# A decoder layer with linear attention and a 32-expert MoE: splits of weights moved into earlier phases, the bias product in one pass, row tiles turned in their own chunk

## The chip, the cores and the metric

The program runs on one core of one Trainium2 chip. The metric is the time of one execution on the device, in microseconds (us); a run's time is compared with the times of the kernel before. Engines: TensorE (matmul and transposes), VectorE (DVE), ScalarE (ACT), GpSimd (POOL), SyncE (SP, which issues transfers).

## What is computed

One layer over 2048 tokens of width 1024, all in float32. After a modulation by a condition vector there is a mixer with gated linear attention and retention heads, then a top-4-of-32 mixture of experts:

```python
h = rmsnorm(x, norm1) * (1 + sc1) + sh1
x = x + g1 * hybrid_mixer(h, ...)          # ends in  o @ w_out
h = rmsnorm(x, norm2) * (1 + sc2) + sh2
logits = hf @ w_router + b_router
top_val, top_idx = lax.top_k(logits, TOP_K)
weights = jax.nn.softmax(top_val)
gate, up = split(xs @ w_gu[e] + b_gu[e])
act = (clip(up, -7, 7) + 1) * (min(gate, 7) * sigmoid(1.702 * min(gate, 7)))
out = (act @ w_down[e] + b_down[e]) * weight      # added to the token's row
x = x + g2 * y;  return rmsnorm(x, norm_f)
```

## The kernel before

Five phases run one after the other, each a block with a program for every engine, and between two phases the semaphores are cleared behind a barrier: modulation, projection (`phase_projection`), mixer (`phase_mixer`), routing (`phase_routing`), experts (`phase_experts`), and a finish. A product of two float32 matrices is made of three matmuls over rounded parts (`split_product`, L113 to L115): hi by hi, hi by lo, lo by hi. ScalarE makes the hi part (a copy to float32r), VectorE the lo part (the value less its hi part).

**Mixer.** 16 turns of 128 tokens. SyncE loads `early` and `late` halves of the projections (L743 to L752) and stores the mixed rows (L757); a late load waits until the tile before last is gated (`out`, L965). VectorE's turn: masks, decayed q and k, `output` of the tile before (L965), state updates (L997, L1004), differences, a reduction (L1011). The output weight w_out is loaded here (L766), 4 MB, and used in the next phase.

**Routing.** First w_out is split: ScalarE four times 128x2048 (L1235), VectorE four times (L1285), with the output norm as factor. Then 16 turns, software-pipelined. TensorE's turn i: product of tile i + 1 with w_out in two halves (L113 to L115), into which are set the transposes of h2 (L1458), the router's product (L1466), the ranks (L1472, L1473) and the transpose of the routing weights W (L1476); then the transposes of tile i + 2's rows (L1436) and the bias product W x b_down (L1483), in plain float32. ScalarE splits the turned rows (L1242), then copies the turned W (L1247). VectorE: x2 from the product (L1340), lo parts (L1301), x added (L1345), yi = bias product x g2 + x2 (L1308, L1309) for the tile before, h2 (L1352, L1354), the list of places (L1314 to L1333), logits and top 4, W. Before the turns it waits for eight setup transfers:

```python
            dve.wait_ge(setup_dma, 8 * 16)
            own(nc.vector.scalar_tensor_tensor(out=A2[:], in0=A2[:], ...
```

POOL stores yi and scatters the places. After the last turn VectorE builds a table of groups (from L1384) and SyncE stores it.

**Experts.** A group is up to four tiles of 128 rows of one expert. SyncE streams its weights in 24 pieces of 512 KB (L1623) through eight buffers: six chunks (four of w_gu, two of w_down) of four pieces. ScalarE and VectorE split each piece (L1689, L1782). TensorE runs chunk by chunk, and in a chunk tile by tile, eight slices of three matmuls each. POOL gathers the rows of the next group (L1644). TensorE turns them (`rows`, L1901, eight transposes into one pair of banks), ScalarE and VectorE split them (L1694, L1788). The first row tile of the next group is turned in chunk 4, two others in the first tile of chunk 5, the fourth behind it:

```python
                                    if c == NGU + 1 and t == 0 and s in (1, 6):
                                        next_rows(s // 4 + 1)
```

At the start of the phase four pieces are split and all tiles of the first group (three here) turned one after the other before the first product.

## Time and profile before

| | |
|---|---|
| median of 3 runs | 4271.72 us (4270.05 to 4272.08) |
| the profiled execution | 4266.8 us, its span 4265.2 us |
| TensorE, VectorE, ScalarE, POOL busy | 93%, 56%, 36%, 14% of the span |
| granted TensorE clock, mean | 0.965 of full speed |
| mixer, routing, experts begin at | 749, 966, 1343 us; the finish at 4212 us |
| weight pieces split in the experts | 840, so 35 groups of 24 |
| transfers | 763 MB, 179 GB/s over the span |

A busy TensorE is not one at its peak, since the ends of matmuls are modelled. The granted clock has two levels, 1.0 (2.4 GHz) and 0.5 (1.2 GHz); a number between them is the mean over a stretch. Durations are of this one profiled execution.

### The profile page before, as it was taken

The page shows a single profiled execution, that of the slowest core. Times are in us where ns is not written, and L with a number is a line of the kernel's source. Part 1 is how long each engine was busy: PE and PEld are TensorE (multiplying, and loading weights), DVE is VectorE, ACT ScalarE, POOL GpSimd, SP SyncE. Part 2 cuts the span into 40 slices and gives each one's busy share as a digit, 9 for nine tenths or more (in the row PEclk, how much of TensorE's full clock was granted, in tenths as well). Part 3 has the DMA queues.
Part 4 walks back from the last instruction along what each step waited for, and adds up shares of the span by engine and source line. Part 5 has one row for each costly group of instructions (what it writes and reads, how often), then busy time and mean ns, then how long its engine had stood idle before and what let it go on. Part 6 is the DMA issues. An engine that isn't in the chain of part 4 may idle for free. (4 is left out here: it accounts for less than half of the span.)

```text
span 4265.2 us, 64554 instructions
## 1 busy us (share of the span) xinstructions
PE 3946.6 (93%) x18376; PEld 3224.3 (76%) x18377; DVE 2371.9 (56%) x3651; ACT 1525.0 (36%) x2203; POOL 590.1 (14%) x616
## 2 busy tenths in 40 slices
PE   6998999897994999999999999999999999999993
PEld 4887788785773877877887878877888788888773
DVE  4262342685665575464476476576556566544653
ACT  3222321562211353342245254355334434322432
POOL 1110110001222110110121011021011111110101
PEclk8999999998996999999999999999999999999997
DMA  5432441653224586464588477588567667544735
GB/s 216 166 112 95 145 146 59 236 202 131 104 94 145 151 262 221 133 213 138 150 260 266 118 261 241 178 264 283 174 192 230 188 193 235 173 128 113 248 111 182
DMA packets 340786, 763.09 MB, mean 179 GB/s; under 512 B 29274, under 2 KB 29332, under 8 KB 336068
## 3 DMA queue, kind: packets, MB, share of 16 engines
q1 hardware_dynamic: 279972, 591.52, 40.6%
q0 software_dynamic: 57680, 160.07, 14.3%
q10 hardware_dynamic: 3056, 10.53, 0.6%
q8 instruction: 41, 0.67, 0.1%
q14 instruction: 37, 0.30, 0.0%
HBM read 653.68 MB, written 108.33 MB: 179 GB/s over the span
## 5 line engine op out<-in xcount | busy, mean ns | idle before, releaser
L1689 ACT CAST exp_w_hi<-exp_w_raw 128x1024 fp32r<-128x1024 f32 x840 | 861.2, 1051 | 943.3 <-PE exp_bank_acc L115 834.7
L113 PE MATMUL exp_bank_acc<-exp_w_hi,exp_x_hi 128*128 128x512 f32 x2528 | 999.7, 395 | 14.4 <-DVE exp_w_lo L1782 12.2
L1782 DVE TENSOR_TENSOR exp_w_lo<-exp_w_raw,exp_w_hi 128x1024 fp32r<-128x1024 f32 x840 | 978.4, 1217 | 59.0 <-ACT exp_w_hi L1689 52.7
L115 PE MATMUL exp_bank_acc<-exp_w_hi,exp_x_lo 128*128 128x512 f32 x2528 | 988.2, 391 | 0.0
L114 PE MATMUL exp_bank_acc<-exp_w_lo,exp_x_hi 128*128 128x512 f32 x2528 | 987.4, 391 | 0.0
L113 PEld LDWEIGHTS exp_bank_acc<-exp_w_hi,exp_x_hi 128*128 128x128 f32 x2528 | 476.7, 189 | 115.9 <-issue 15.5
L115 PEld LDWEIGHTS exp_bank_acc<-exp_w_hi,exp_x_lo 128*128 128x128 f32 x2528 | 476.4, 188 | 101.6
L114 PEld LDWEIGHTS exp_bank_acc<-exp_w_lo,exp_x_hi 128*128 128x128 f32 x2528 | 477.3, 189 | 95.7
L113 PE MATMUL exp_bank_acc<-exp_w_hi,exp_a_hi 128*128 128x512 f32 x1264 | 506.7, 401 | 12.6 <-DVE exp_a_lo L1840 9.3
L115 PE MATMUL exp_bank_acc<-exp_w_hi,exp_a_lo 128*128 128x512 f32 x1264 | 493.6, 391 | 0.0
L114 PE MATMUL exp_bank_acc<-exp_w_lo,exp_a_hi 128*128 128x512 f32 x1264 | 493.2, 390 | 0.0
L1671 POOL DMA_INDIRECT y_rows<-exp_act_row,exp_token x123 | 196.2, 1595 | 2117.1 <-DVE exp_act_row L1852 2073.6
L113 PE MATMUL pro_bank_acc<-pro_w_hi,pro_h_hi 128*128 128x512 f32 x896 | 355.8, 397 | 0.0
L115 PE MATMUL pro_bank_acc<-pro_w_hi,pro_h_lo 128*128 128x512 f32 x896 | 350.9, 392 | 0.0
L114 PE MATMUL pro_bank_acc<-pro_w_lo,pro_h_hi 128*128 128x512 f32 x896 | 350.8, 392 | 0.0
L113 PEld LDWEIGHTS exp_bank_acc<-exp_w_hi,exp_a_hi 128*128 128x128 f32 x1264 | 237.8, 188 | 71.9 <-DVE exp_a_lo L1840 21.7
L1816 DVE SCALAR_TENSOR_TENSOR exp_gate_up<-exp_bank_acc,exp_bias 128x512 f32<-128x512 f32 x158 | 108.9, 689 | 319.2 <-PE exp_bank_acc L115 318.7
L1852 DVE SCALAR_TENSOR_TENSOR exp_act_row<-exp_bank_acc,exp_share,exp_g 128x512 f32<-128x512 f32 x123 | 92.0, 748 | 331.0 <-PE exp_bank_acc L115 322.6
L115 PEld LDWEIGHTS exp_bank_acc<-exp_w_hi,exp_a_lo 128*128 128x128 f32 x1264 | 237.5, 188 | 51.0
L114 PEld LDWEIGHTS exp_bank_acc<-exp_w_lo,exp_a_hi 128*128 128x128 f32 x1264 | 238.1, 188 | 44.9
L1805 DVE TENSOR_TENSOR exp_gate_up<-exp_bank_acc,exp_bias 128x512 f32<-128x512 f32 x158 | 108.5, 686 | 262.5 <-PE exp_bank_acc L115 116.2
L1713 ACT CAST exp_a_hi<-exp_bank_ta 128x512 fp32r<-128x512 f32 x158 | 92.5, 585 | 452.2 <-PE exp_bank_ta L1909 452.2
(299 smaller groups left out, 4286.3 us busy)
## 6 DMA issues: line engine op xcount, KB each, us to landing
exp_w_raw<-in_w_gu SPq DMA_DIRECT2D x560, 512.0 KB
exp_w_raw<-in_w_down SPq DMA_DIRECT2D x280, 512.0 KB
exp_bias<-in_b_gu SPq DMA_DIRECT2D x35, 1024.0 KB
early_w_raw<-in_w_in POOLq DMA_DIRECT2D x14, 2048.0 KB, 10.8
proj<-pro_stage SPq DMA_DIRECT2D x112, 256.0 KB
pro_w_ada<-in_w_ada POOLq DMA_DIRECT2D x64, 256.0 KB, 3.3
mix_late<-proj SPq DMA_DIRECT2D x16, 768.0 KB, 6.2
mod_w_ada<-in_w_ada SPq DMA_DIRECT2D x8, 1024.0 KB, 15.8
```

Of the source, the lines that this page charges most:

```text
L113: nc.tensor.matmul(out, act_hi, w_hi, start=first, stop=False)
L114: nc.tensor.matmul(out, act_hi, w_lo, start=False, stop=False)
L115: return nc.tensor.matmul(out, act_lo, w_hi, start=False, stop=last)
L1671: pool.indirect_dma_start(out=keep["y"][c - NGU], out_offset=bass.IndirectOffsetOnAxis(ap=token[:, t:t + 1], axis=0), in_=weighted_at(c, t ...
L1689: nc.scalar.copy(whi[:, c % 2, j * SK:(j + 1) * SK], raw[:, n % RAW]).then_inc(hi_done, 1)
L1713: nc.scalar.copy(ahi[:, t, 4 * q:4 * q + 4], ta[:]).then_inc(ahi_done, 1)
L1782: nc.vector.tensor_tensor(wlo[:, c % 2, rows], raw[:, n % RAW], whi[:, c % 2, rows], ALU.subtract).then_inc(lo_done, 1)
L1805: nc.vector.tensor_tensor(gu[:, t % 2], acc[:, bank(c, t)], bias[:, column(c):column(c) + N], ALU.add).then_inc(read_done, 1)
L1816: nc.vector.scalar_tensor_tensor(out=gu[:, u], in0=acc[:, bank(c, t)], scalar=1.0, in1=bias[:, column(c):column(c) + N], op0=ALU.add, op1= ...
L1852: nc.vector.scalar_tensor_tensor(out=weighted_at(c, t), in0=acc[:, bank(c, t)], scalar=share[:, t:t + 1], in1=g2[:, cols], op0=ALU.mult, o ...
```

## The change

1. The split of w_out moves from the head of the routing into the mixer: after each of the 16 turns ScalarE makes one hi piece of 128x512 and VectorE, at the end of its next turn, the lo piece. Raw and split weights lie in tiles that routing and experts share.
2. b_down is loaded three times, one below the other, and held as hi, lo, hi (`b_down_split`, float32r); W is held as hi, hi, lo. The bias product is two matmuls of 96 rows, in float32r. W's turned copy goes ahead of the row split on ScalarE.
3. SyncE loads the first eight weight pieces of expert 0 in the routing, behind its last loads; four are split there, around the last turn. Expert 0 always counts as one tile at least, so that group 0 is expert 0's. The eight first pieces of each next expert are then loaded at the end of a group's list.
4. yi and the places' records have two buffers; the last list of places goes ahead of the last yi.
5. In the experts only the first row tile is turned ahead; the others in the first chunk of their own group, tile t + 1 after the first slice of tile t.
6. One clearing of semaphores goes.

The core of the diff:

```diff
+def pieces_of(raw):
+    return raw[:].rearrange("p a s n -> p (a s) n").rearrange("p (r s) n -> p r s n", s=SK)
+def expert_piece(A, expert, n):
+    c, rows = n // PIECES, slice(n % PIECES * SK, (n % PIECES + 1) * SK)
+    w, col = (A["w_gu"], (c % 2) * D + (c // 2) * N) if c < 4 else (A["w_down"], (c - 4) * N)
+    return w.rearrange("o e (s p) n -> p (o e) s n", p=P)[:, bass.ds(expert, 1), rows, col:col + N]
...
+            for n in range(2):
+                for c in range(2):
+                    sp.dma_start(w_out[:, n, c * GH:(c + 1) * GH], rows_of(A["w_out"])[:, n * GH:(n + 1) * GH, c * N:(c + 1) * N]
+                                 ).then_inc(w_out_in, 16)
...
+                act.wait_ge(w_out_in, 6 * 16)
+                at = bass.ds(j, 1)
+                nc.scalar.activation(w_hi[:, u, at], w_out[:, u, at], ACT.Identity, scale=o_norm[:, u:u + 1]
+                                     ).then_inc(w_hi_done, 1)
...
+                if not is_tile(i, 0):
+                    out_weights_lo(i - 1, 1 - u, j - 1 + u)
+            def out_weights_lo(t, u, j):
+                dve.wait_ge(w_hi_done, t + 1)
+                at = bass.ds(j, 1)
+                nc.vector.scalar_tensor_tensor(out=w_lo[:, u, at], in0=w_out[:, u, at], scalar=o_norm[:, u:u + 1],
+                                               in1=w_hi[:, u, at], op0=ALU.mult, op1=ALU.subtract).then_inc(w_lo_done, 1)
...
+    bd3 = k.sb("b_down_split", [3 * E, D], F32R)
...
-            sp.dma_start(bd[:], A["b_down"].rearrange("o e d -> (o e) d")).then_inc(setup_dma, 16)
+            for part in range(3):
+                sp.dma_start(bd[part * E:(part + 1) * E, :], A["b_down"].rearrange("o e d -> (o e) d")).then_inc(setup_dma, 16)
...
+            for n in range(RAW):
+                sp.dma_start(raw[:, n], expert_piece(A, 0, n)).then_inc(first_in, 16)
...
-            for c in range(2):
-                act.wait_ge(w_in, 64)
-                for n in range(2):
-                    rows = slice(n * GH, (n + 1) * GH)
-                    ins = nc.scalar.activation(whi[:, c, rows], raw[:, c, rows], ACT.Identity, scale=keep["o_norm"][:, n:n + 1])
-                ins.then_inc(whi_done, 1)
+            def first_weights_hi(n):
+                act.wait_ge(first_in, RAW * 16)
+                nc.scalar.copy(first[:, 0, n * SK:(n + 1) * SK], raw[:, n]).then_inc(first_hi, 1)
...
+                if not is_tile(i, 0):
+                    weights_t(i - 1)
                 if not is_tile(i, NT - 1):
                     split_hi(i + 1)
-                if not is_tile(i, 0):
-                    weights_t(i - 1)
...
+                if is_tile(i, NT - 1):
+                    for n in range(2):
+                        first_weights_hi(n)
...
+            act.wait_ge(setup_dma, 10 * 16)
+            nc.scalar.copy(bd3[:], bd).then_inc(bd_hi, 1)
...
-            for c in range(2):
-                dve.wait_ge(whi_done, c + 1)
-                for n in range(2):
-                    rows = slice(n * GH, (n + 1) * GH)
-                    ins = nc.vector.scalar_tensor_tensor(out=wlo[:, c, rows], in0=raw[:, c, rows], scalar=keep["o_norm"][:, n:n + 1],
-                                                         in1=whi[:, c, rows], op0=ALU.mult, op1=ALU.subtract)
-                ins.then_inc(wlo_done, 1)
-            own(nc.vector.memset(empty[:], 0))
+            own(nc.vector.memset(empty, 0))
...
-            dve.wait_ge(setup_dma, 8 * 16)
+            dve.wait_ge(setup_dma, 10 * 16)
             own(nc.vector.scalar_tensor_tensor(out=A2[:], in0=A2[:], scalar=1.0, in1=norm2[:], op0=ALU.add, op1=ALU.mult))
             dve.wait_ge(pool_set, 1)
+            dve.wait_ge(bd_hi, 1)
+            lo = slice(E, 2 * E)
+            nc.vector.tensor_tensor(bd3[lo], bd[lo], bd3[lo], ALU.subtract).then_inc(bd_lo, 1)
...
-                nc.vector.tensor_scalar(W[:], W[:], den[:], None, ALU.mult).then_inc(ev["W"], 1)
+                own(nc.vector.tensor_scalar(W[:], W[:], den[:], None, ALU.mult))
+                own(nc.vector.tensor_copy(W3[:, 0:2], W[:].unsqueeze(1).to_broadcast([P, 2, E])))
+                nc.vector.tensor_tensor(W3[:, 2], W[:], W3[:, 0], ALU.subtract).then_inc(ev["W"], 1)
             split_lo(0)
             for_tiles(dve, step)
             own.base, own.n = SETUP + NT * PER - BEFORE, 0
+            list_places(NT - 1, 1)
             first_rows(NT - 1, 1)
-            list_places(NT - 1)
...
+            for count in (tiles, groups):
+                fin(nc.vector.tensor_scalar(count[:, 0:1], count[:, 0:1], 1.0, None, ALU.max))
...
+            for n in range(2, PIECES):
+                first_weights_lo(n)
+            dve.wait_ge(first_lo, PIECES)
...
-                nc.tensor.transpose(wt[0:E, 0:P], W[:], ident).then_inc(ev["wt"], 1)
+                nc.tensor.transpose(wt[0:3 * E, 0:P], W3[:].bitcast(F32).rearrange("p a e -> p (a e)"), ident
+                                    ).then_inc(ev["wt"], 1)
...
-                                          bd[:, c * N:(c + 1) * N], start=True, stop=True)
+                                          bd3[:, c * N:(c + 1) * N], start=True, stop=True)
...
+                    for n in range(RAW, PIECES * NCH):
+                        load(n, expert)
+                    next_expert = field(sp, g + 1, EXPERT, E - 1)
+                    with sp.If(G.nT > 0):
+                        for n in range(PIECES * NCH, PIECES * NCH + RAW):
+                            load(n, next_expert)
...
-            for n in range(PIECES):
-                weights_hi(0, n, 1)
-            T0 = tiles_in(load_word(act, 0))
-            for t in range(GT):
-                with act.If(T0 > t):
-                    rows_hi(0, t)
+            rows_hi(0, 0)
...
                     for n in range(PIECES, 2 * PIECES + PIECES // 2):
+                        if n % 2 == 0 and n // 2 - 1 < GT:
+                            own_rows_hi(n // 2 - 1)
                         weights_hi(g, n, G.chunks_before(n // PIECES - 1))
...
+                            if c == 0 and n % 2 == 0:
+                                own_rows_lo(n // 2 + 1)
                             weights_lo(g, PIECES * (c + 1) + n)
+                        if c == 0:
+                            own_rows_lo(3)
...
-                                            next_rows(0)
+                                            next_row()
                                     if c == NGU and s == KD // 2:
                                         pe.wait_ge(alo_done, G.pair_tile(1, t))
-                                    if c == NGU + 1 and t == 0 and s in (1, 6):
-                                        next_rows(s // 4 + 1)
+                                    if c == 0 and s == 1 and t + 1 < GT:
+                                        own_rows(t + 1)
...
-            kw = Kit(nc, mixing, "w_out")
-            keep["w_out"], keep["w_out_in"] = kw.sb("raw", [P, 2, KD, N]), kw.sem("in")
-            keep["o_norm"] = kw.sb("o_norm", [P, 2])
+            kw = Kit(nc, mixing, "weights")
+            keep["raw"] = kw.sb("raw", [P, 2, KD, N])
+            keep["split"] = kw.sb("split", [P, 4, KD, N], F32R)
             run(phase_mixer)
+            keep["first"] = kw.sb("first", [P, 2, KD, N], F32R)
             run(phase_routing)
-            kw.clear_sems()
-        run(phase_experts)
+            run(phase_experts)
...
```

**VectorE, end of the mixer and head of the routing.** (`weights_split` is the split w_out, `rou_A` is A2.) Before:

```order
L1011 TENSOR_REDUCE mix_var<-mix_sq 128x4
L965 SCALAR_TENSOR_TENSOR mix_o_out<-mix_oc,mix_r,mix_late 128x128 x8
L725 UNCONDITIONAL_BRANCH
L1278 UNCONDITIONAL_BRANCH
L1285 SCALAR_TENSOR_TENSOR rou_w_lo<-w_out_raw,w_out_o_norm,rou_w_hi 128x2048 x4
L1288 MEMSET rou_empty 128x1024
L1289 TENSOR_SCALAR rou_col<-keep_const 128x1
L1290 CAST rou_empty<-rou_col 128x512
L1292 SCALAR_TENSOR_TENSOR rou_A<-rou_A,rou_norm 128x1024
L1301 TENSOR_TENSOR rou_o_lo<-rou_bank_tp,rou_o_hi 128x512 x2
```

Changed:

```order
L1037 TENSOR_REDUCE mix_var<-mix_sq 128x4
L1044 SCALAR_TENSOR_TENSOR weights_split<-weights_raw,mix_o_norm,weights_split 128x512 x2
L991 SCALAR_TENSOR_TENSOR mix_o_out<-mix_oc,mix_r,mix_late 128x128 x8
L744 UNCONDITIONAL_BRANCH
L1328 UNCONDITIONAL_BRANCH
L1331 MEMSET rou_yi 128x1024
L1332 TENSOR_SCALAR rou_col<-keep_const 128x1
L1333 CAST rou_yi<-rou_col 128x512
L1335 SCALAR_TENSOR_TENSOR rou_A<-rou_A,rou_h 128x1024
L1339 TENSOR_TENSOR rou_b_down_split<-rou_yi,rou_b_down_split 32x1024
L1352 TENSOR_TENSOR rou_o_lo<-rou_bank_tp,rou_o_hi 128x512 x2
```

The two last lo pieces now stand ahead of the mixer's last output, the four large ones are gone, and the bias's low part is new between A2 and the first row split.

**ScalarE, a turn in the routing's loop.** Before:

```order
L1242 CAST rou_o_hi<-rou_bank_tp 128x512 x2
L1245 REGISTER_ALU
L1246 REGISTER_ALU
L1247 COPY rou_wT<-rou_bank_wt 32x128
L1256 ACTIVATE rou_squares,rou_ssq<-rou_x 128x1024
```

Changed:

```order
L1289 CAST rou_wT<-rou_bank_wt 96x128
L1281 REGISTER_ALU
L1282 REGISTER_ALU
L1284 CAST rou_o_hi<-rou_bank_tp 128x512 x2
L1298 ACTIVATE rou_over,rou_ssq<-rou_x 128x1024
```

The copy of the turned W, which the bias product needs, went ahead of the row split.

**TensorE, first tile of a group's last chunk (before) and of its first chunk (changed).** Before:

```order
L1927 COMPARE_AND_BRANCH
L1931 ISA
L1901 MATMUL exp_bank_tx<-keep_const,exp_rows 128x128 x8
L1927 UNCONDITIONAL_BRANCH
L113 MATMUL exp_bank_acc<-exp_w_hi,exp_a_hi 128x512
```

Changed:

```order
L116 MATMUL exp_bank_acc<-weights_first,weights_split 128x512
L117 MATMUL exp_bank_acc<-weights_first,weights_split 128x512
L118 MATMUL exp_bank_acc<-weights_first,weights_split 128x512
L1998 COMPARE_AND_BRANCH
L1968 MATMUL exp_bank_tx<-keep_const,exp_rows 128x128 x8
L1998 UNCONDITIONAL_BRANCH
L116 MATMUL exp_bank_acc<-weights_first,weights_split 128x512
```

A turn of rows that stood among the products of the activations, twice there and once behind them, now stands after the first slice of a tile's first product (the operands named `weights_split` there are the rows' parts).

## Rows read from the trace of the kernel before

**Rows 1.** Windows of TensorE: stretch, its length, busy, granted clock, DMA share, GB/s
```profile
985.00:1299.00 314.00, 289.70 (x1380) 0.94 0.26 94
...
1085.00:1105.00 20.00, 18.70 (x90) 0.91 0.30 103
```

**Rows 2.** TensorE's waits over the span: us in total, times, longest
```profile
PE exp_bank_acc L113 <- DVE exp_w_lo L1782: 14.9, 14, 1.6
...
PE mix_bank_go L1084 <- DMA mix_late<-proj: 8.6, 9, 2.3
...
PE exp_bank_tx L1901 <- DVE exp_x_lo L1788: 6.8, 6, 2.0
```

**Rows 3.** Groups by line: count, busy us, mean ns of one, idle before
```profile
L115 PE MATMUL exp_bank_acc<-exp_w_hi,exp_x_lo 128*128 128x512 f32 x2528 | 988.2, 391 | 0.0
...
L1483 PE MATMUL rou_bank_tq<-rou_b_down,rou_wT 32*128 32x512 f32 x64 | 34.6, 662 | 19.0 <-ACT rou_wT L1247 19.0
...
L1285 DVE SCALAR_TENSOR_TENSOR rou_w_lo<-w_out_raw,w_out_o_norm,rou_w_hi 128x2048 fp32r<-128x2048 f32 x4 | 9.1, 2346 | 9.2 <-ACT rou_w_hi L1235 9.2
```

**Rows 4.** Order of time in the mixer: start us, length us, what [idle before]
```profile
827.35 1.43 DVE L997 SCALAR_TENSOR_TENSOR mix_gla_state<-mix_gla_state,mix_eb,mix_bank_gs 64x128 f32<-64x128 f32 x4 [3.16 <-PE mix_bank_gs L1103]
...
835.31 2.18 DVE L965 SCALAR_TENSOR_TENSOR mix_o_out<-mix_oc,mix_r,mix_late 128x128 f32<-128x128 f32 x8
...
838.42 0.33 SPq L751 DMA_DIRECT2D mix_late<-proj  x1
...
845.08 0.70 PE L1084 MATMUL mix_bank_go<-mix_gla_state,mix_qe 128*128 128x256 f32 x2 [0.66 <-DMA mix_late<-proj]
...
850.67 1.43 DVE L997 SCALAR_TENSOR_TENSOR mix_gla_state<-mix_gla_state,mix_eb,mix_bank_gs 64x128 f32<-64x128 f32 x4 [1.88 <-PE mix_bank_gs L1103]
```

**Rows 5.** Order of time in the routing
```profile
970.66 0.71 SPq L1193 DMA_DIRECT2D rou_norm<-in_norm  x1
...
984.78 0.76 PE L113 MATMUL rou_bank_acc<-rou_w_hi,rou_o_hi 128*128 128x512 f32 x1 [12.90 <-issue]
...
1016.73 1.23 DVE L1340 TENSOR_TENSOR rou_x<-rou_bank_acc,rou_g 128x1024 f32<-128x1024 f32 x1 [3.86 <-PE rou_bank_acc L115]
...
1020.88 1.23 DVE L1308 TENSOR_TENSOR rou_yi<-rou_bank_tq,rou_g 128x1024 f32<-128x1024 f32 x1 [0.25 <-PE rou_bank_tq L1483]
...
1024.60 1.23 DVE L1354 TENSOR_TENSOR rou_h<-rou_h,rou_sh 128x1024 f32<-128x1024 f32 x1
...
1036.31 1.22 DVE L1340 TENSOR_TENSOR rou_x<-rou_bank_acc,rou_g 128x1024 f32<-128x1024 f32 x1 [3.87 <-PE rou_bank_acc L115]
...
1299.03 1.23 DVE L1340 TENSOR_TENSOR rou_x<-rou_bank_acc,rou_g 128x1024 f32<-128x1024 f32 x1 [3.81 <-PE rou_bank_acc L115]
```

**Rows 6.** Order of time on VectorE, tail of the routing
```profile
1320.25 1.23 DVE L1308 TENSOR_TENSOR rou_yi<-rou_bank_tq,rou_g 128x1024 f32<-128x1024 f32 x1 [4.61 <-PE rou_bank_tq L1483]
...
1326.56 0.69 DVE L1384 TENSOR_TENSOR rou_over<-rou_run,keep_const 128x512 f32<-128x512 f32 x1
...
1336.99 0.17 DVE L1426 CAST rou_table_i<-rou_table 128x6 int32<-128x6 f32 x1
```

**Rows 7.** Order of time on TensorE, start of the experts and one group's end
```profile
1363.61 1.97 PE L1901 MATMUL exp_bank_tx<-keep_const,exp_rows 128*128 128x128 f32 x8 [32.72 <-DMA exp_rows<-h_rows,exp_next_token]
...
1371.55 1.97 PE L1901 MATMUL exp_bank_tx<-keep_const,exp_rows 128*128 128x128 f32 x8 [2.00 <-DVE exp_x_lo L1788]
...
1374.27 0.79 PE L113 MATMUL exp_bank_acc<-exp_w_hi,exp_x_hi 128*128 128x512 f32 x1 [0.76 <-issue]
...
2322.58 0.76 PE L113 MATMUL exp_bank_acc<-exp_w_hi,exp_x_hi 128*128 128x512 f32 x1 [1.55 <-DVE exp_w_lo L1782]
```

**Rows 8.** Transfers by line: count, KB each, us from issue to landing
```profile
exp_rows<-h_rows,exp_next_token POOLq DMA_INDIRECT x79, 8.2
...
rou_norm<-in_norm SPq DMA_DIRECT2D x1, 512.0 KB, 9.7
```

**Rows 9.** Windows of all engines: busy of PE, PEld, DVE, ACT, POOL, clock, DMA share, GB/s
```profile
976.00:978.00 2.00, 0.00 (x0) 0.00 (x0) 2.00 (x1) 0.07 (x1) 0.00 (x0) 0.50 1.04 414
```

198 lines of the change are left out of this document (104 added, 94 removed).

## The prediction

> **What bounds the kernel now.** I read the busy time by stage first. In the routing's steady part TensorE is busy 290 of 314 us [rows 1], and in the experts, from 1374 us on, nearly always. Time can therefore come from three places: a wait of TensorE, a seam in which it has nothing to do, or work of its own that goes away. Its list of waits comes next [rows 2]: in the mixer it waits 9 times, 8.6 us in all, for late projections from memory, in the experts for VectorE's split of weights (14.9 us) and of rows (6.8 us). The groups by line [rows 3] show the bias product: 34.6 us in 64 records, four to a tile, and 19.0 us of idle time ahead of it. Last, the order of time at the seams [rows 4 to 7] shows what ends each gap.
>
> **Mixer: + 5.0 us.** Each turn gets one more op on ScalarE and one on VectorE, 128x512. VectorE's four old splits took 2.35 us per 128x2048 [rows 3], so a piece costs 0.6. VectorE is in a loop here: state update at 827.35, output gated by 837.49, its end lets SyncE issue the late load at 838.42, whose landing ends TensorE's wait at 845.08, and the state update after that is at 850.67 [rows 4]. That is 10.1 + 7.6 + 5.6 = 23.3 us for two turns. The new op stands between the state update and the output, so this loop gets 0.6 longer: 7 loops and a bit, + 4.4. At the end two new ops (1.2 us) stand ahead of the last output, where I reckon with one of them hidden behind ScalarE's roots: + 0.6. ScalarE's op goes behind its last copies of a turn, where it waits for VectorE's differences; if that cover went, it would delay the exponentials by 0.6 a turn. Bounds: 0, if the load were not in the loop, to 16 x 0.6 = 9.6.
>
> **Start of the routing: + 1.3 us, not a gain.** Before, TensorE starts its first product at 984.78 [rows 5], behind the splitting of the output weights that now is gone. But VectorE's queue has, ahead of the first split of a row tile, a wait for all setup transfers. The last of them (norm2) is issued at 970.66 [rows 5] and takes 9.7 us [rows 8]: 980.4. At 976 to 978 the transfers run at 414 GB/s [rows 9]. Two more copies of the down bias (0.25 MB) and the 0.5 MB that clear the places, issued well over 10 us earlier since VectorE is free, come ahead: + 1.9 us, 982.3. Behind the wait stand A2, the new low part of the bias (1024 columns each, 1.23 [rows 5]) and the row split, 1.3: 986.0. Bounds: - 0.6 if the extra bytes hide, + 3 if they queue worse. What is moved into the mixer is thus paid there and not earned here.
>
> **Routing's turns: - 8 us.** From the second to the last tile (1016.73 to 1299.03, 14 turns) a turn takes 20.16 us; one at full clock takes 19.58 (1016.73 to 1036.31) [rows 5]. The bias product becomes two matmuls of a kind that is recorded at 391 ns, instead of four at 662 [rows 3], and its weights are copied ahead of the row split on ScalarE, so the wait of 19.0 / 15 = 1.3 us a tile goes. It cannot all be earned: the next product waits for the row split anyway, and then VectorE's chain from the product (1016.73) through x2, yi and h2 (done at 1025.83) holds the transposes of h2. In that chain only the wait for the bias product goes, 0.25 us [rows 5]. What TensorE gains it will mostly spend waiting for h2. So a turn becomes 19.58 - 0.25 = 19.33, and the slow turns lose their excess too, since TensorE has slack where its clock now falls (0.91 granted over 1085 to 1105 [rows 1], a stretch at 1.2 GHz right behind the wait and the bias product): 14 x (20.16 - 19.33) = 11.6. I give back two dips in 14 turns that fall in work instead, at 1.8 us each (20 us x 0.09), which leaves 8. Bounds: - 12 to + 12 (below).
>
> **Tail of the routing: - 3.9 us.** VectorE idles 4.61 us for the last bias product and starts yi at 1320.25; the list of places follows and the table begins at 1326.56 [rows 6]. Now the list (3.8 us) goes into that idle time and yi (2.45) behind it, and the table begins some 4.1 us earlier. New in the chain are two maxima, at 0.2 each as the small row of [rows 6]: + 0.4. Four weight pieces are split here as well: ScalarE's four and VectorE's first two lie in idle time ahead of the logits, VectorE's last two (2.45) run while the table's store lands, perhaps 0.3 past it; one clearing of semaphores with its barrier is gone, an estimate of - 0.5. Bounds: - 2 to - 5.
>
> **Start of the experts: - 9.5 us.** The gathered rows land at 1363.61 and the first product starts at 1374.27, after three tiles were turned one by one [rows 7]. The eight weight pieces (4 MB) ahead of the gathers are now loaded in the routing; the bias and four pieces stay ahead, 3 MB. With 1.5 MB of rows at 0.4 MB/us from 1348 that ends at 1359.5, - 4.1. And only one tile is turned before the first product: 2.7 us (1371.55 to 1374.27) in place of 10.66, less 2.4 for the two turned inside, - 5.5. Bounds: - 5 to - 13.
>
> **Turns of the experts: - 11 us.** Of the 6.8 us for row splits 4.0 are those of the start (2.00 twice [rows 7]); the other 2.8 stand mostly at the ends of four groups of one tile, which turn two or three next tiles in their last chunk, and each is followed by 1.55 for weights [rows 7]: 2.8 + 6.2 = 9. Another 2 I take for other waits for weights at group starts and for clock dips behind these waits. The turning itself (8 transposes a tile) is moved, not saved. New waits: tile t + 1 is turned one slice into tile t, so ScalarE and VectorE have the other seven slices, 21 matmuls, for their 2.7 us of work; I take nothing. POOL's fetch for the next group now waits for the last own tile, still three chunks early. SyncE's loads keep their order. Bounds: - 4 to - 16.
>
> **Sum.** 5.0 + 1.3 - 8 - 3.9 - 9.5 - 11 = - 26.1 us. The profiled execution took 4266.8 us, so 4240.7; it lies 4.9 below the median of the runs, 4271.7, which gives 4245.6. I say **4245**.
>
> **Rivals.** (a) *The bias product is earned in full*: 34.6 - 32 x 0.391 = 22 us of TensorE's work go, and if TensorE is the limit, the routing's turns give - 22 in place of - 8: 4231. For: it is 92% busy there. Against: h2's chain. 0.13. The Trainium skill ("FP8 and Floating Point Precision", TensorE Precision Notes) says that true FP32 takes four passes through the array; by that rule alone three quarters of the product, 26 us, would go and the time be 4227. The four records a tile (two halves, two records each) show passes, though not four for each matmul. (b) *The clock falls in every turn*: two idle pieces (row split, h2) drop it to 1.2 GHz in the work behind h2: 14 x 1.8 = 25 us in place of 3.6, so 4267. For: it falls in most turns now. Against: no idle piece is longer than today's. 0.12. The Trainium skill ("TensorE: Matmul & The Clock Gate", A second HAM failure mode) describes such alternation where TensorE idles briefly between groups of matmuls; the trace agrees, at 0.91. (c) *Own tiles wait*: 79 tiles [rows 8] in 35 groups make 44 own tiles. If ScalarE or VectorE is held by weight pieces when one is turned, TensorE waits in the first chunk, each time. From 0.8 us a tile (35 us) it eats the gain and more; at 1.2 it is 53, 4298, slower. Against: both engines are half idle. 0.04. (d) *The early load does not help*, since the gather itself is the limit, and the mixer pays its full 9.6: 4255. 0.09. The forecast has 0.62.
>
> **Numbers.** A measurement of this kernel can tell some 0.2% from no change, 8.5 us. Faster: the forecast, (a), (d), 0.84, and the better edge of (b), 0.87; same: (b), 0.10; slower: (c), 0.03. The range goes from (a) with a margin to short of (b): 4227 to 4264.
>
> **What would show it.** Right: waits for the late load some 4 us larger; the first product no sooner after the routing's start than before; turns of 19.3 us with waits for h2 of 1 to 2 us; the list of places ahead of yi in the tail; one tile turned before the first expert product; no wait for row splits at group ends. Wrong: turns over 20 us with the clock at 0.9 behind h2, waits for exp_x_lo in first chunks, or a mixer 10 us longer.

## The result, and the profile after

The changed kernel took 4242.66 us, median of 5 runs (4239.17 to 4248.45); the kernel before took 4270.05 in the runs beside it. The ratio is 0.9939, with a 95% interval of 0.9926 to 0.9952: 27.4 us or 0.6% faster, 2.3 us from the forecast of 4245. The profiled execution has a span of 4243.0 us, 22.2 less than the 4265.2 of before. By seams (the same event in both traces; "before" and "changed" are lengths in us):

| from, to | forecast | before | changed | moved |
|---|---|---|---|---|
| start, end of the mixer's last output | + 5.0 | 962.19 | 968.84 | + 6.65 |
| to the first product of the routing | + 1.3 | 22.59 | 24.43 | + 1.84 |
| to the second x2 | 0 | 31.95 | 32.23 | + 0.28 |
| second to last x2, 14 turns | - 8 | 282.30 | 270.67 | - 11.63 |
| last x2 to the cast of the table | - 3.9 | 37.96 | 34.18 | - 3.78 |
| cast to the first expert product | - 11.9 | 37.28 | 29.28 | - 8.00 |
| first to last expert product | - 8.6 | 2825.22 | 2820.02 | - 5.20 |
| to the end | 0 | 65.7 | 63.3 | - 2.4 |

The forecast had charged the start of the experts (- 9.5) with the 2.4 us of turning two tiles that moved into their first chunk; by seams this belongs to the experts, so - 11.9 and - 8.6 stand in the table. Its - 3.9 for the tail also holds two small terms that by seams lie behind the cast (+ 0.3 for weight pieces, - 0.5 for the clearing of semaphores), so it said - 3.7 for that row. The sums are - 26.1 forecast and - 22.2 measured; the profiled execution took 4244.65 us, where the forecast's sum gave it 4240.7.

TensorE's windows over the routing (first product to last x2, and one steady turn; columns as in [rows 1]):

```profile
993.00:1296.00 303.00, 259.40 (x1352) 0.98 0.30 110
1085.00:1105.00 20.00, 16.16 (x87) 1.00 0.30 111
```

It was busy 92% there before and is busy 86% now, at a higher granted clock. Its waits over the span, to be read against [rows 2]:

```profile
PE exp_bank_acc L116 <- DVE weights_first L1849: 12.4, 16, 1.3
PE mix_bank_go L1119 <- DMA mix_late<-proj: 12.1, 12, 2.0
...
PE exp_bank_acc L116 <- DVE weights_split L1849: 2.8, 2, 2.3
PE exp_bank_acc L116 <- DVE weights_split L1855: 2.1, 1, 2.1
```

The waits for the late load grew by 3.5 us, those for row splits shrank from 6.8 + 1.3 to 2.1 (the first tile of all), and those for weights stayed (14.9 before, 12.4 + 2.8 now). The bias product by line, and the two new ops of the mixer:

```profile
L1548 PE MATMUL rou_bank_tq<-rou_b_down_split,rou_wT 96*128 96x512 f32 x32 | 11.8, 451 | 0.4 <-ACT rou_wT L1289 0.4
...
L1044 DVE SCALAR_TENSOR_TENSOR weights_split<-weights_raw,mix_o_norm,weights_split (+1 forms) x16 | 11.8, 742 | 0.0
L921 ACT ACTIVATE weights_split<-weights_raw,mix_o_norm (+1 forms) x16 | 11.7, 734 | 0.0
```

34.6 us of TensorE's recorded busy time became 11.8, and 19.0 us of idle time ahead of it 0.4. A piece of the weights takes VectorE 0.74, where the forecast had 0.6.

The mixer's loop, in order of time (to be read against [rows 4]):

```profile
865.80 1.43 DVE L1023 SCALAR_TENSOR_TENSOR mix_gla_state<-mix_gla_state,mix_eb,mix_bank_gs 64x128 f32<-64x128 f32 x4 [1.18 <-PE mix_bank_gs L1138]
...
869.93 0.74 DVE L1044 SCALAR_TENSOR_TENSOR weights_split<-weights_raw,mix_o_norm,weights_split  x1
...
874.43 2.18 DVE L991 SCALAR_TENSOR_TENSOR mix_o_out<-mix_oc,mix_r,mix_late 128x128 f32<-128x128 f32 x8
...
877.55 0.33 SPq L770 DMA_DIRECT2D mix_late<-proj  x1
...
885.01 0.70 PE L1119 MATMUL mix_bank_go<-mix_gla_state,mix_qe 128*128 128x256 f32 x2 [1.63 <-DMA mix_late<-proj]
...
890.60 1.43 DVE L1023 SCALAR_TENSOR_TENSOR mix_gla_state<-mix_gla_state,mix_eb,mix_bank_gs 64x128 f32<-64x128 f32 x4 [2.19 <-PE mix_bank_gs L1138]
```

The new piece stands between the state update and the output, and the output's end (876.6) still sets the late load (877.55) and with it TensorE's wait and the state update after it. This loop of two turns took 24.80 us, where that of [rows 4] took 23.32; over the whole mixer, 7.5 such loops, the mean one grew by 0.5 (3.7 / 7.5).

The routing's start on ScalarE, VectorE and TensorE, to be read against the 984.78 of [rows 5]:

```profile
978.38 1.07 ACT L1284 CAST rou_o_hi<-rou_bank_tp 128x512 fp32r<-128x512 f32 x2 [4.25 <-PE rou_bank_tp L1499]
...
989.42 1.23 DVE L1335 SCALAR_TENSOR_TENSOR rou_A<-rou_A,rou_h 128x1024 f32<-128x1024 f32 x1 [14.79 <-DMA rou_h<-in_norm]
...
991.92 1.29 DVE L1352 TENSOR_TENSOR rou_o_lo<-rou_bank_tp,rou_o_hi 128x512 fp32r<-128x512 f32 x2
...
993.27 0.80 PE L116 MATMUL rou_bank_acc<-weights_split,rou_o_hi 128*128 128x512 f32 x1 [14.92 <-DVE rou_o_lo L1352]
```

VectorE idles 14.79 us for the last setup transfer while the row's high parts, ready at 979.45, wait for their low parts behind it. One steady turn has two waits of TensorE, for the row split and for h2, which replace that for the turned W:

```profile
1028.33 0.50 PE L116 MATMUL rou_bank_acc<-weights_split,rou_o_hi 128*128 128x512 f32 x1 [1.53 <-DVE rou_o_lo L1352]
...
1034.31 1.09 PE L1522 MATMUL rou_bank_tq<-keep_const,rou_h 128*128 128x128 f32 x8 [1.53 <-DVE rou_h L1406]
```

The routing's tail on VectorE, against [rows 6]: yi has no wait ahead of it any more, and the table begins 23.4 us after the last x2 instead of 27.5.

```profile
1317.14 1.22 DVE L1360 TENSOR_TENSOR rou_yi<-rou_bank_tq,rou_g 128x1024 f32<-128x1024 f32 x1
...
1319.54 0.68 DVE L1441 TENSOR_TENSOR rou_over<-rou_run,keep_const 128x512 f32<-128x512 f32 x1
...
1330.35 0.17 DVE L1486 CAST rou_table_i<-rou_table 128x6 int32<-128x6 f32 x1
```

The start of the experts, against [rows 7]: last gather issued, rows turned, first product, on POOL and TensorE.

```profile
1345.20 0.94 POOL L1707 DMA_INDIRECT exp_rows<-h_rows,exp_next_token  x1 [0.30 <-issue]
...
1355.53 1.97 PE L1968 MATMUL exp_bank_tx<-keep_const,exp_rows 128*128 128x128 f32 x8 [31.28 <-DMA exp_rows<-h_rows,exp_next_token]
...
1359.63 0.80 PE L116 MATMUL exp_bank_acc<-weights_first,weights_split 128*128 128x512 f32 x1 [2.13 <-DVE weights_split L1855]
```

### The profile page after: what moved, and what is told of

It reads as the page before. It is cut to its first block and busy times, and to the rows that moved or that the text cites. A ratio compares the mean times of both kernels' runs of the same rounds, so it can differ in the third digit from the quotient of the medians.

```text
span 4243.0 us, 64683 instructions
## 1 busy us (share of the span) xinstructions
PE 3914.0 (92%) x18344; PEld 3210.0 (76%) x18345; DVE 2382.9 (56%) x3698; ACT 1525.5 (36%) x2216; POOL 570.0 (13%) x616
## 5 line engine op out<-in xcount | busy, mean ns | idle before, releaser
L1757 ACT CAST weights_split<-weights_raw 128x1024 fp32r<-128x1024 f32 x420 | 431.8, 1055 | 538.2 <-PE exp_bank_acc L118 489.7
L116 PE MATMUL exp_bank_acc<-weights_first,weights_split 128*128 128x512 f32 x1264 | 505.9, 400 | 9.7 <-DVE weights_first L1849 7.2
L1849 DVE TENSOR_TENSOR weights_split<-weights_raw,weights_split 128x1024 fp32r<-128x1024 f32 x420 | 490.6, 1219 | 26.4 <-ACT weights_split L1757 19.4
L116 PE MATMUL exp_bank_acc<-weights_split 128*128 128x512 f32 x1264 | 497.8, 394 | 2.8 <-DVE weights_split L1849 2.8
L118 PE MATMUL exp_bank_acc<-weights_split 128*128 128x512 f32 x1264 | 494.9, 392 | 0.0
L117 PE MATMUL exp_bank_acc<-weights_split 128*128 128x512 f32 x1264 | 494.8, 391 | 0.0
L118 PE MATMUL exp_bank_acc<-weights_first,weights_split 128*128 128x512 f32 x1264 | 494.3, 391 | 0.0
L117 PE MATMUL exp_bank_acc<-weights_first,weights_split 128*128 128x512 f32 x1264 | 493.6, 391 | 0.0
L1849 DVE TENSOR_TENSOR weights_first<-weights_raw,weights_first 128x1024 fp32r<-128x1024 f32 x416 | 483.4, 1218 | 14.6 <-ACT weights_first L1757 14.5
L1757 ACT CAST weights_first<-weights_raw 128x1024 fp32r<-128x1024 f32 x416 | 425.4, 1050 | 161.7 <-PE exp_bank_acc L118 129.0
L116 PEld LDWEIGHTS exp_bank_acc<-weights_first,weights_split 128*128 128x128 f32 x1264 | 238.0, 188 | 60.3 <-issue 12.0
L116 PEld LDWEIGHTS exp_bank_acc<-weights_split 128*128 128x128 f32 x1264 | 239.4, 189 | 53.5 <-DVE weights_split L1849 4.3
L118 PEld LDWEIGHTS exp_bank_acc<-weights_split 128*128 128x128 f32 x1264 | 239.0, 189 | 50.6
L117 PEld LDWEIGHTS exp_bank_acc<-weights_split 128*128 128x128 f32 x1264 | 239.1, 189 | 49.3
L118 PEld LDWEIGHTS exp_bank_acc<-weights_first,weights_split 128*128 128x128 f32 x1264 | 237.8, 188 | 50.9
L117 PEld LDWEIGHTS exp_bank_acc<-weights_first,weights_split 128*128 128x128 f32 x1264 | 238.5, 189 | 45.1
## 6 DMA issues: line engine op xcount, KB each, us to landing
early_w_raw<-in_w_in POOLq DMA_DIRECT2D x14, 2048.0 KB, 10.9
```

The lines of the kernel that those rows point to most:

```text
L116: nc.tensor.matmul(out, act_hi, w_hi, start=first, stop=False)
L117: nc.tensor.matmul(out, act_hi, w_lo, start=False, stop=False)
L118: return nc.tensor.matmul(out, act_lo, w_hi, start=False, stop=last)
L1757: nc.scalar.copy(whi[c % 2][:, j * SK:(j + 1) * SK], raw[:, n % RAW]).then_inc(hi_done, 1)
L1849: nc.vector.tensor_tensor(wlo[c % 2][:, rows], raw[:, n % RAW], whi[c % 2][:, rows], ALU.subtract).then_inc(lo_done, 1)
```

## The experiments

Twelve kernels ran, each beside runs of the kernel before on the same chip. Runs of one kernel scatter by up to 10 us to either side of their median, so a median can settle some 10 us. Most seams of a profile settle one; the mixer and the experts scatter by more, as shown below. The table gives, per kernel: median; ratio to before with its interval; mixer from the first to the last state update; from the last state update to the first product of the routing; mean turn from the second to the last x2; from the cast of the table to the first expert product; first to last expert product.

| kernel | median | ratio | mixer | start | turn | experts' start | experts |
|---|---|---|---|---|---|---|---|
| before (its first profile) | 4270.05 | 1 | 176.9 | 28.3 | 20.16 | 37.3 | 2825.2 |
| changed | 4242.66 | 0.9939 (0.9926 to 0.9952) | 180.6 | 30.8 | 19.33 | 29.3 | 2820.0 |
| after_again | 4245.36 | 0.9947 (0.9933 to 0.9960) | 179.3 | 30.6 | 19.32 | 29.3 | 2824.7 |
| lo_behind_output | 4241.20 | 0.9935 (0.9922 to 0.9947) | 174.7 | 29.9 | 19.38 | 28.9 | 2827.4 |
| wout_in_routing | 4239.37 | 0.9931 (0.9920 to 0.9943) | 173.2 | 29.6 | 19.36 | 29.4 | 2822.1 |
| row0_first | 4235.55 | 0.9920 (0.9907 to 0.9933) | 179.7 | 18.2 | 19.38 | 29.0 | 2824.2 |
| before_row0_first | 4263.60 | 0.9990 (0.9981 to 0.9999) | 173.4 | 25.4 | 20.43 | 37.4 | 2824.5 |
| bias_in_fp32 | 4244.61 | 0.9945 (0.9932 to 0.9959) | 180.6 | 30.5 | 19.33 | 29.4 | 2823.9 |
| copy_behind_split | 4244.26 | 0.9953 (0.9938 to 0.9968) | 178.2 | 30.9 | 19.33 | 28.6 | 2814.9 |
| bias_as_before | 4261.64 | 0.9989 (0.9980 to 0.9998) | 180.9 | 30.7 | 20.33 | 28.1 | 2824.1 |
| late_first_load | 4245.89 | 0.9952 (0.9938 to 0.9965) | 177.1 | 30.8 | 19.32 | 28.8 | 2817.3 |
| gathers_first | 4240.18 | 0.9940 (0.9925 to 0.9956) | 176.6 | 30.5 | 19.33 | 24.5 | 2823.8 |
| rows_as_before | 4256.23 | 0.9976 (0.9967 to 0.9985) | 179.2 | 30.7 | 19.33 | 34.9 | 2824.4 |
| three_moves | 4223.77 | 0.9902 (0.9887 to 0.9917) | 176.1 | 17.4 | 19.33 | 24.4 | 2823.9 |

### How well a profile repeats

> The changed kernel, unchanged, for a comparison on the same chip and a second profile. Theory on the scatter: the seams repeat within 1 us (turns of 19.33, first expert product 4.1 us after the rows), while the mixer's length (176.6 to 180.6 us from the first to the last state update in the profiles so far) and the experts (2815 to 2827) do not, because a few falls of the clock land differently; median 4240 to 4246.

The median is 4245.36, the span 4243.7. The mean turn and the start of the experts repeat to 0.02 us; the mixer differs by 1.3, the experts by 4.6. The experts' scatter over these kernels (2814.9 to 2827.4) is mostly no wait: in the two that lie furthest apart, copy_behind_split and lo_behind_output, TensorE's waits there sum to 60.9 and 62.5 us, while its busy time for the same 12630 recorded matmuls is 2752.8 and 2763.9 us. What differs is the clock. In that stretch of the two profiles the granted clock is at its lower level for 13.4 us (three times) and 40.5 us (eleven times):

```profile
1354.82:4169.70 2814.88, 2753.83 (x12632) 1.00 0.63 196
```

```profile
1352.77:4180.15 2827.38, 2764.91 (x12632) 0.99 0.63 195
```

If work at 1.2 GHz takes twice its time, which is an estimate, half of that time is lost: 6.7 and 20.3 us, and the difference of 13.6 covers the 12.5 us between the seams. Taken off in the same way in every profile, the eleven with the new order of rows lie at 2806.7 to 2809.4 us (mean 2807.8) and the three with the old order at 2811.8, 2813.0 and 2813.2 (mean 2812.7). So what lies within 5 us in the experts is not read from the seam of one profile as it stands, but with the clock taken off 2 us can be.

### The output weights: mixer and start of the routing

lo_behind_output moves one call, VectorE's piece, from the end of a step to right behind the output:

```diff
                     output(i - 1, 1 - u, j - 1 + u)
+                    out_weights_lo(i - 1, 1 - u, j - 1 + u)
...
                 nc.vector.tensor_reduce(var[:, GH:2 * GH], sq[:, GH:2 * GH], AX_X, ALU.add).then_inc(ev["red"], 1)
-                if not is_tile(i, 0):
-                    out_weights_lo(i - 1, 1 - u, j - 1 + u)
```

> The changed kernel, with VectorE's piece of the output weights in the mixer put right behind the output of a tile, where VectorE idles 0.4 to 2 us for the state's product, instead of between the state update and the next output. My theory (a loop through VectorE, SyncE's late load and TensorE; two turns took 23.3 us before and 23.9 now): the loop returns to 23.3, the mixer is 4 to 5 us shorter, 4238. Rival: the mixer is longer by the 0.6 of the op wherever it stands, or by ScalarE's op or the weights' transfers: no change.

The order of time on VectorE in its mixer:

```profile
872.06 2.18 DVE L991 SCALAR_TENSOR_TENSOR mix_o_out<-mix_oc,mix_r,mix_late 128x128 f32<-128x128 f32 x8
...
874.15 0.75 DVE L1043 SCALAR_TENSOR_TENSOR weights_split<-weights_raw,mix_o_norm,weights_split  x1
...
875.39 1.43 DVE L1024 SCALAR_TENSOR_TENSOR mix_gla_state<-mix_gla_state,mix_eb,mix_bank_gs 64x128 f32<-64x128 f32 x4 [0.49 <-PE mix_bank_gs L1137]
```

The piece now takes idle time: 0.49 us is still left ahead of the state update. The mixer took 174.7 us (176.1 in three_moves, which has the same order; mean 175.4). Nine profiles with the piece inside the loop gave 176.6 to 180.9, mean 179.1; three with no piece in the mixer 173.2 to 176.9, mean 174.5. So splitting in the mixer cost 4.6 us, and the place of VectorE's piece alone 3.7 of them. The 0.9 that is left for the rival (ScalarE's op, the piece wherever it stands) is less than the scatter of these few profiles. The median moved by 1.5 only, within its scatter; the medians would not show it, the averages of the seams do.

wout_in_routing undoes the whole first part: the mixer keeps only the transfers, and the four old pieces run at the start of the routing (shown for VectorE; ScalarE's stand likewise ahead of its first split, and the product waits for `w_lo_done`; the output norm is kept beside the constants):

```diff
             own = Steps(dve, dve_step)
+            for c in range(2):
+                dve.wait_ge(w_hi_done, c + 1)
+                for n in range(2):
+                    rows = slice(c * GH, (c + 1) * GH)
+                    ins = nc.vector.scalar_tensor_tensor(out=w_lo[:, n, rows], in0=w_out[:, n, rows], scalar=o_norm[:, n:n + 1],
+                                                         in1=w_hi[:, n, rows], op0=ALU.mult, op1=ALU.subtract)
+                ins.then_inc(w_lo_done, 1)
             own(nc.vector.memset(empty, 0))
```

> The changed kernel with its first part undone: the output weights are split at the start of the routing, as before (four pieces of 2048 columns on ScalarE and VectorE). My theory: the mixer takes 6 us less and the first product starts as long after the mixer's last state update as in the changed kernel (30.8 us), since the wait for the setup transfers ends later than the weights: 5 to 6 us less than the changed kernel, 4237. Rival: the first part pays for itself, and without it the start of the routing is later by what the weights take, so that the sum is the same or up to 4 us more.

The mixer is at 173.2, and the first product comes 29.6 us after the last state update, 1.2 sooner than in the changed kernel. The median is 3.3 us lower, 4 by the span; that is within the scatter, and the sign comes from the average of the mixer (4.6) and from this seam (1.2). Moved to the mixer in this way, the splitting was a small loss, as forecast, since it was not what the first product waited for. row0_first shows what was (`split_lo_first` is `split_lo` for tile 0):

```diff
             nc.vector.tensor_copy(empty[:, :, 0], col[:, 0:1].to_broadcast([P, PLACES])).then_inc(empty_set, 1)
+            split_lo_first()
             dve.wait_ge(setup_dma, 10 * 16)
...
-            split_lo(0)
             for_tiles(dve, step)
```

> The changed kernel, but VectorE splits the first row tile of the routing ahead of its wait for the setup transfers instead of behind it. My theory: that wait, not the output weights, set the first product in the changed kernel (993.27; the setup landed at 989.42, the high parts of the row were ready at 979.5). The product then starts at about 981.5, the first x2 at 994.6 instead of 1006.5, and all that follows moves with it: 11 to 12 us less than the changed kernel, 4231. Rival: the start is only moved, because the first h2 then waits for the same transfers (A2, shift), or the second row tile does: under 4 us less.

On VectorE and TensorE:

```profile
978.96 1.29 DVE L1335 TENSOR_TENSOR rou_o_lo<-rou_bank_tp,rou_o_hi 128x512 fp32r<-128x512 f32 x2 [4.69 <-ACT rou_o_hi L1284]
...
990.13 1.22 DVE L1343 SCALAR_TENSOR_TENSOR rou_A<-rou_A,rou_h 128x1024 f32<-128x1024 f32 x1 [9.88 <-DMA rou_h<-in_norm]
...
980.31 0.80 PE L116 MATMUL rou_bank_acc<-weights_split,rou_o_hi 128*128 128x512 f32 x1 [2.00 <-DVE rou_o_lo L1335]
```

The product starts at 980.31 instead of 993.27 and the last x2 comes at 1283.81 instead of 1296.17: 12.4 us, since VectorE's wait for the setup (9.88) now lies beside the first product. The second tile is not held either, so the rival falls. The median is 7.1 lower, 8.5 by the span: of the 12.4, 4.1 went into an experts' stage of 2824.2 instead of 2820.0, which is the usual value.

> The kernel before, with the same move (the first row tile is split behind the four weight pieces and ahead of the places and the wait for the setup transfers). My theory: here the weight pieces end at 980.5 and hold the product, so the product goes from 984.78 to 982, 2.5 to 3 us less than before (4267); the output weights' place in the mixer is worth 10 us at this seam only together with the move. Rival: if the setup transfers held it here too, the gain would be as large as in the changed kernel, some 11 us.

In the kernel before, the same call right behind its four weight pieces gave 2.9 us at the seam (28.3 to 25.4) and 4.2 by the medians (4267.77 for before in these runs), at a ratio whose interval ends at 0.9999. The two halves need each other: weights split in the mixer and the row split ahead of the wait give a start of 18.2 us; the move alone 25.4, the weights alone 30.8.

### The bias product

bias_in_fp32 makes W, its turned copy and the bias fp32 again, 32 rows deep (the three-part layout is still filled, two parts unused), and keeps ScalarE's order. copy_behind_split keeps the product and swaps `weights_t(i - 1)` and `split_hi(i + 1)` back. bias_as_before has both edits.

```diff
-                                          bd3[:, c * N:(c + 1) * N], start=True, stop=True)
+                                          bd3[0:E, c * N:(c + 1) * N], start=True, stop=True)
```

```diff
-                if not is_tile(i, 0):
-                    weights_t(i - 1)
                 if not is_tile(i, NT - 1):
                     split_hi(i + 1)
+                if not is_tile(i, 0):
+                    weights_t(i - 1)
```

> The changed kernel with the bias product back in fp32 (32 rows deep, fp32 operands), its weights still copied ahead of the row split. My theory: TensorE has 3.3 us of waits in each 19.4-us turn since VectorE's chain sets the turn, so the 1.9 us more that the product takes per tile (4 records of 662 ns for 2 of 391) hide in the wait for the row split almost wholly: turns of 19.4 to 19.6, the seam from the second to the last x2 0 to 3 us longer than the changed kernel's 270.7, and no measurable change of the time (4242 to 4246). Rival: the product's format is what made the turns shorter, and they go back to 20.1: 11 us slower than the changed kernel, 4253.

> The changed kernel with only ScalarE's order undone: the turned W is copied behind the split of the next row tile, so that the bias product waits for it as before (1.3 us a tile). My theory: at full clock a turn is 0 to 0.25 us longer (the wait of VectorE for the bias product), 0 to 3 us in all; if the falls of the clock come back too (they stood behind this wait), turns of 20 us and 10 us in all. Rival: only the format counts, and this order changes nothing at all (19.33 to 19.4 a turn).

> The changed kernel with both parts of the bias product undone (fp32 format, and the turned W copied behind the row split). Each alone left the turns at 19.33. Theory: each alone ends the product before VectorE asks for it, so only both together bring back VectorE's wait (0.25 us a turn, 19.58 at full clock) and with it the falls of the clock: turns of 19.6 to 20.2, the seam from the second to the last x2 3.5 to 12 us longer than 270.7, the time 4246 to 4254. Rival: the turns got shorter for another reason (yi in two buffers, POOL's order of places and rows), and stay at 19.33.

Turns of 19.33, 19.33 and 20.33. Of bias_in_fp32 and then of copy_behind_split, TensorE in one turn:

```profile
1087.32 0.50 PE L116 MATMUL rou_bank_acc<-weights_split,rou_o_hi 128*128 128x512 f32 x1 [0.24 <-DVE rou_o_lo L1352]
...
1093.41 1.06 PE L1522 MATMUL rou_bank_tq<-keep_const,rou_h 128*128 128x128 f32 x8 [1.65 <-DVE rou_h L1406]
```

```profile
1088.39 1.07 PE L1522 MATMUL rou_bank_tq<-keep_const,rou_h 128*128 128x128 f32 x8 [1.64 <-DVE rou_h L1406]
...
1100.93 0.73 PE L1548 MATMUL rou_bank_tq<-rou_b_down_split,rou_wT 96*128 96x512 f32 x2 [1.32 <-ACT rou_wT L1289]
```

With the long product, TensorE's wait for the row split shrinks from 1.53 to 0.24; with the late copy, the wait of 1.32 takes its place. Either alone fits into the slack that VectorE's chain leaves, and TensorE waits 1.65 for h2 either way. That settles the rival of the full gain: over 21 us of TensorE's recorded busy time went, and by itself that is worth nothing.

On the price of fp32, the Trainium skill ("FP8 and Floating Point Precision", TensorE Precision Notes) gives four passes. The busy time here fell from 33.5 us to 11.8, a factor of 2.8, but the modelled lengths overlap and say little. From start to start the traces agree with the page: at full clock two fp32 records stand 429 ns apart (bias_in_fp32), so a matmul of two records takes 858 ns, and the split matmuls of the same 512 columns in the experts stand 227 ns apart (median), a factor of 3.8. For the time of the kernel neither number mattered.

With both back, TensorE and VectorE read so, and the windows around the first of these rows show the granted clock (columns: stretch, length, busy, clock, DMA share, GB/s):

```profile
1046.23 2.94 PE L1548 MATMUL rou_bank_tq<-rou_b_down_split,rou_wT 32*128 32x512 f32 x4 [1.40 <-ACT rou_wT L1289]
...
1090.44 1.23 DVE L1360 TENSOR_TENSOR rou_yi<-rou_bank_tq,rou_g 128x1024 f32<-128x1024 f32 x1 [0.26 <-PE rou_bank_tq L1548]
```

```profile
1046.00:1048.00 2.00, 1.77 (x3) 0.78 0.09 33
1048.00:1050.00 2.00, 2.00 (x4) 0.50 0.41 98
1050.00:1052.00 2.00, 2.00 (x6) 0.50 1.01 389
1052.00:1054.00 2.00, 2.00 (x7) 0.52 0.09 37
```

VectorE's wait of 0.26 is back (19.58 for a turn at full clock), and the clock falls to 1.2 GHz for 3.4 or 6.8 us, behind the idle piece and in or right behind the long product: six times in the 13 turns from 1030 to 1280, nine times in the same stretch of the kernel before, seven times in before_row0_first. But falls do not need that pair. The changed kernel has two there, each for 3.4 us behind a wait of 1.68 us for the row split and with no long product, the first here:

```profile
1048.00:1050.00 2.00, 2.00 (x7) 0.57 0.10 18
```

Its second profile, lo_behind_output, wout_in_routing, late_first_load and rows_as_before have two as well, row0_first has three, and gathers_first and three_moves, with the same turns, have none before the last x2. There the turn hides them, as TensorE has slack: in the changed kernel every second turn takes 19.46 or 19.47 us, with a fall or without. In the kernel before, a turn with a fall of 3.4 us took 20.2 to 20.3 us and one with 6.8 us 21.8, against 19.58. That bias_in_fp32 and copy_behind_split had none is read from one profile each, and so lies within what kernels with the same turns show. What is shown is that with both edits back there are more falls, and that they lie in work that the turn waits for; why the clock falls is not.

The seam from the second to the last x2 is 284.6 us against 270.7: 14 us, and 16 by the medians (against the 4245.36 of the same chip). So 3.5 us of it are VectorE's wait (14 turns of 0.25), and the other 10 stand in the turns with a fall.

The busy share of the whole stretch does not tell the kernels apart: bias_in_fp32 is busy 91% of that stretch (227.5 of 250 us) at a clock of 1.00, the kernel before 93% at 0.93. The Trainium skill ("TensorE: Matmul & The Clock Gate", A second HAM failure mode) describes a clock that goes up and down where TensorE idles briefly between groups of matmuls. The traces agree in so far as each of the 37 falls that begin in this stretch, over all profiles, began 0.4 to 3.0 us after the end of an idle piece of 1.3 to 1.8 us. But copy_behind_split has idle pieces of 1.3 and 1.6 us in every turn and no fall in that stretch, so such a piece alone does not bring one each time.

### The start of the experts

late_first_load loads expert 0's eight pieces at the start of the experts, ahead of the bias, and splits the first chunk there (`weights_hi(0, n, 1)` and `weights_lo(0, n)` ahead of the first rows):

```diff
             sp.wait_ge(word_set, 1)
+            for n in range(RAW):
+                sp.dma_start(raw[:, n], expert_piece(A, 0, n)).then_inc(raw_in[n], 16)
             count = field(sp, 0, COUNT, NG)
```

gathers_first adds one wait to SyncE ahead of its loop:

```diff
             sp.wait_ge(word_set, 1)
+            sp.wait_ge(tx_done, 2)
             count = field(sp, 0, COUNT, NG)
```

> The changed kernel with the early load undone: expert 0's first eight weight pieces are loaded at the start of the experts, ahead of the bias, and its first chunk split there, as before. The rows landed 9.3 us after the last gather was issued with and without these 4 MB ahead, and 3.9 us after it once nothing was ahead. Theory: with them ahead the bias and the second chunk move behind the gathers, so the rows land at most 1.5 us later; the early load is worth 0 to 2 us, 4243 to 4245. Rival: it is worth the 4 us that the prediction gave it, 4247.

> The changed kernel with SyncE holding the first group's bias and second-chunk weights (3 MB in all) until the first row tile is turned. In both kernels the rows landed 9.3 us after the last gather was issued, with 4 MB less ahead of it in the changed one. My theory: the transfers that are issued just ahead of the gathers still hold them; without them the rows land 4 to 5 us after the last issue (4.2 is the shortest landing of a gather elsewhere in this trace), the first product is 4 to 5 us earlier, and the second chunk's weights still arrive in time (17 us later): 4 us less than the changed kernel, 4238. Rival: the gathers themselves take the 9.3 us (1.5 MB in small rows), nothing is gained, and the weights of the second chunk come late: the same or up to 3 us slower.

Of late_first_load, then of gathers_first: last gather on POOL, first turning and first product on TensorE.

```profile
1340.35 1.52 POOL L1694 DMA_INDIRECT exp_rows<-h_rows,exp_next_token  x1 [0.30 <-issue]
...
1350.29 1.97 PE L1957 MATMUL exp_bank_tx<-keep_const,exp_rows 128*128 128x128 f32 x8 [30.94 <-DMA exp_rows<-h_rows,exp_next_token]
...
1354.25 0.80 PE L116 MATMUL exp_bank_acc<-weights_first,weights_split 128*128 128x512 f32 x1 [2.00 <-DVE weights_split L1842]
```

```profile
1338.73 0.94 POOL L1708 DMA_INDIRECT exp_rows<-h_rows,exp_next_token  x1 [0.30 <-issue]
...
1343.63 1.97 PE L1969 MATMUL exp_bank_tx<-keep_const,exp_rows 128*128 128x128 f32 x8 [26.47 <-DMA exp_rows<-h_rows,exp_next_token]
...
1347.73 0.79 PE L116 MATMUL exp_bank_acc<-weights_first,weights_split 128*128 128x512 f32 x1 [2.13 <-DVE weights_split L1856]
```

From the last gather's issue to the first turning (these starts): changed 10.3 us, late_first_load 9.9, gathers_first 4.9. The early load is worth nothing at this seam (28.8 without it, 29.3 with it), and the medians agree. The orders of issue say why. In the kernel before, then in late_first_load, the bias and the four pieces behind it are issued only after the last gather (which starts at 1353.26 and at 1340.35):

```profile
1353.96 0.35 SPq L1618 DMA_DIRECT2D exp_bias<-in_b_gu  x1
```

```profile
1340.97 0.36 SPq L1666 DMA_DIRECT2D exp_bias<-in_b_gu  x1
```

In the changed kernel the bias is issued at 1340.35 and the fourth piece at 1343.30, while the gathers start at 1342.60 to 1345.20. So with the first eight pieces (4 MB) gone, these 3 MB moved up and took their place ahead of the rows. Held back altogether, they free 4.8 us (24.5), and they are not missed later: the waits for weights in the experts are 14.1 us there, 15.2 in the changed kernel. The median is 2.5 lower, inside the scatter.

rows_as_before undoes the last part in the four engines' programs: tiles of the next group are turned in the last chunk, all tiles of the first group ahead of its first product. On TensorE:

```diff
-                                    if c == 0 and s == 1 and t + 1 < GT:
-                                        own_rows(t + 1)
+                                    if c == NGU + 1 and t == 0 and s in (1, 6):
+                                        next_rows(s // 4 + 1)
```

> The changed kernel with the last part undone: row tiles of the next group are turned in the last chunk of a group, all tiles of the first group ahead of its first product. My theory: rows landed to first product is 10.7 us again instead of 4.1, less the 2.5 us that the turning takes inside, and the four one-tile groups wait for x_lo again (0.7 each) and longer for the next weights: 7 to 11 us slower than the changed kernel, 4251. Rival: in the groups nothing was gained (the waits for weights only moved), so that the start's 4 us remain: 4247.

```profile
1352.31 1.97 PE L1973 MATMUL exp_bank_tx<-keep_const,exp_rows 128*128 128x128 f32 x8 [30.21 <-DMA exp_rows<-h_rows,exp_next_token]
...
1356.28 1.97 PE L1973 MATMUL exp_bank_tx<-keep_const,exp_rows 128*128 128x128 f32 x8 [2.00 <-DVE weights_split L1858]
...
1363.12 0.79 PE L116 MATMUL exp_bank_acc<-weights_first,weights_split 128*128 128x512 f32 x1 [0.91 <-issue]
```

and its list of waits has the old entry back:

```profile
PE exp_bank_tx L1973 <- DVE weights_split L1858: 7.0, 6, 2.0
```

Rows to first product: 10.8 us against 4.1. By the median this part is worth 13.6 us (4256.23 against 4242.66; 10.9 against the second set of runs), by the span 8.5. The start explains 6.7 less the 2.4 that now run inside. In the groups, TensorE's waits are 67.7 us here, 68.3 and 68.6 in the two profiles with the old order besides, and 60.9 to 64.0 in the eleven with the new one (mean 62.0): 6 us. Together 6.7 - 2.4 + 5.7 = 10. With the clock taken off the experts' stage as above it is 6.7 + 5.4 (2813.2 less 2807.8) = 12. The rival (only the start) falls.

### The three moves together

> The changed kernel with three moves together: the first row tile split ahead of the wait for the setup transfers, VectorE's piece of the output weights right behind the output in the mixer, and SyncE's first bias and second chunk held until the first row tile is turned. By the seams of the three runs: 12.4 + 4.4 + 4.4 = 21 us less than the changed kernel; by their medians 7 + 2 + 2.5 = 11 us. Theory: the seams add up, as they lie in different stages: 4220 to 4230. Rival: part of it is given back in the experts, as the single runs' medians seemed to say: 4230 to 4234.

4223.77 us, 18.9 under the changed kernel (21.6 under its second set of runs) and 1.0% under the kernel before. The seams added up: start of the routing 30.8 to 17.4, experts' start 29.3 to 24.4, mixer 179.1 to 176.1: 21 us. Where single runs seemed to lose part of their seam, the combination did not, so that loss was most likely scatter. This is the version to use.

## Why the prediction was right

**Mixer, + 5.0: right, 6.65 in this profile.** The loop was the one named, and its price over nine profiles is 4.6 where 4.4 was said (7 loops by 0.6; the op takes 0.74). The tail was said to be 0.6: from the last state update to the end of the last output it grew from 5.73 to 6.36. What is left of the 6.65 is within the scatter.

**Start of the routing, + 1.3: right, + 1.84, and the mechanism shown.** The wait for all setup transfers stands ahead of the row split, and it ended at 989.42, 10 us after that split could have begun (978.96 in row0_first). The forecast's "paid there and not earned here" held: undoing this part alone took 4.6 us off the mixer (average) and 1.2 off this seam, 3.3 by the medians. What it did not say is how large the gain behind the wait was, 12.4 us, for moving one call.

**Turns, - 8: the sign and the working right, the discount wrong.** VectorE's chain gives 19.33 a turn, as computed, and 14 turns gave 11.63, as computed before I gave back two falls of the clock at 1.8 us. The sentence that failed is "I give back two dips in 14 turns that fall in work instead". In its place, the two falls from 1030 to 1280 left turns of 19.47 us, as long as others without one. And one assumption behind it was only argued: the runs show that either edit alone, the format or the copy's order, gives all of it. The edits are not additive, and counting them by TensorE's work (22 us, or the 26 of rival (a) by four passes) would have been wrong. What that rival says of the records, two to a matmul and so not four passes, does not speak against four: see their distances above.

**Tail, - 3.9: right as far as the cast (- 3.7 said, - 3.78 measured).** 4.1 from the list of places going into VectorE's idle time, 0.4 back for the two maxima (10.43 to 10.81 us from table start to cast).

**Start of the experts, - 9.5: the step on the transfers failed.** It had two parts. One tile turned instead of three: said - 5.5, measured 10.66 to 4.10 us less 2.4, - 4.2. The 2.7 that it put for one tile was read behind the third, whose split the first product need not await; a tile by itself is followed by that wait too (1.97 + 2.13). Eight pieces fewer ahead of the rows: said - 4.1, measured 0. The step was "the bias and four pieces stay ahead, 3 MB. With 1.5 MB of rows at 0.4 MB/us from 1348 that ends at 1359.5": in the old order these 3 MB had stood behind the gathers, so the bytes ahead of them went from 4 MB to 3 and not from 7 to 3, and the last gather landed 10.3 us after its start in both. What the seam did gain besides is 1.4 us from the cast to the first gather's issue (13.66 to 12.26). Over all profiles this stretch is 12.3 to 12.9 with the change and 13.7 and 13.2 without, about 1 us. The clearing of semaphores that is gone may be the cause, but no run undid it alone, and the - 0.5 that the forecast gave it was read from no row.

**Turns of the experts, - 11: mis-sized.** The waits for row splits went, as said. The 1.55 for weights behind each one-tile group did not go but shrank to 0.7, and others stand in the last chunks: in the groups the waits fell by 6 us in all. The seam's - 5.20 (- 7.6 with the 2.4 that moved in, against - 11) is one profile's; with the clock taken off, the means of both orders differ by 4.8, which makes - 7.2. Rival (c), own tiles that wait in the first chunk, did not show: the only wait for a row split in the changed kernel is the first tile's.

**The end, 0: missed by 2.4.** From the last product to the end all twelve profiles with the change have 62.8 to 64.4 us, the kernel before 65.7 and before_row0_first 66.0. Nothing was edited in the finish; 1.9 of it lies between the last accumulation's issue and SyncE's first load of the finish (9.2 to 7.3 us). Its cause wasn't tried.

The forecast's total is close for a reason that is partly luck: it had 4 us too much at the load and 3 in the experts' turns, 4 too little in the routing's turns and 2 at the end.

## What to carry to other kernels

When work is taken out from ahead of a seam, look in the same queue for what stands next: here a wait for all setup transfers held the first product for 12 us, and one call moved ahead of it won them. Two repairs of one wait are not added: undo each alone, and then both, before crediting either. Put an added piece where its engine idles inside the loop, not merely where the data are ready; and when bytes are taken from ahead of a transfer, ask what moves up into their place. Before a stage's length in one profile is compared with another's, take off what the clock cost in each.

## What the runs showed of the hardware

TensorE's clock fell to 1.2 GHz for 3.4 or 6.8 us at a time. In the 13 turns of the routing from 1030 to 1280 us the three profiles with an idle piece of 1.3 to 1.4 us and the fp32 product behind it had nine, seven and six falls; the other eleven had none to three, and of two kernels with the same code in that phase one had two (the changed kernel) and one none (gathers_first). Each of these 37 falls began 0.4 to 3.0 us after the end of an idle piece of 1.3 to 1.8 us; most such pieces had no fall behind them. The busy share of that stretch did not tell them apart: 91% at a mean clock of 1.00 (bias_in_fp32, 227.5 of 250 us), 91% at 0.94 (bias_as_before, 228.6). In bias_as_before the turns with falls made up 10 us in 14 turns; in the changed kernel falls cost nothing, since TensorE waits in each turn anyway.

In the experts the time at 1.2 GHz differed from profile to profile, 13.4 to 40.5 us of 2820, and half of it, an estimate, accounts for the scatter of that stage but for 3 us.

The rows of three tiles were in 4.0 us after the end of their last issue when SyncE's weights were held back (1339.67 to 1343.63 in gathers_first), and 9.4 us after it in the changed kernel with 3 MB issued ahead. With 4 MB issued ahead and 3 MB right behind the last gather it was 9.4 in the kernel before (1354.21 to 1363.61) and 8.4 in late_first_load.
